# Choosing experts by top-eight and index instructions, and a new order for the last token tile of a router

## The reference

```
x = x + mix @ w_out
xn2 = rmsnorm(x, norm2_g)
lg = xn2 @ rg_w + rg_b                      # 8 groups
grp = top_k(lg, 1)
le = (xn2 @ re_w + re_b).reshape(t, 8, 8)   # 64 experts
top_v, top_i = top_k(le[grp], 2)
gate = softmax(lg)[grp] * softmax(top_v)
eidx = grp * 8 + top_i
x = x + sum over the two of gate * expert(eidx, xn2)
y = rmsnorm(x, final_norm_g)
```

## Time and profile before

| | us |
|---|---|
| median of three runs | 1886.19 (1886.02 to 1888.94) |
| span of the profiled execution | 1886.5 |
| PE busy in the span | 1759.1 (93%) |
| VectorE, ScalarE, GpSimd busy | 598.8, 444.0, 230.5 |
| moved by DMA | 406.33 MB, 215 GB/s over the span |

### The profile page before, as it was taken

One profiled execution on the slowest core, in us unless ns is written; L12 is line 12 of the kernel. 1 busy time (PEld: TensorE's weight loads), 2 busy tenths in 40 slices (PEclk: granted clock), 3 DMA queues, 4 the chain that ended last, 5 costly groups with the idle time before them and its releaser, 6 DMA issues.

```text
span 1886.5 us, 27617 instructions
## 1 busy us (share of the span) xinstructions
PE 1759.1 (93%) x11500; PEld 1479.2 (78%) x11500; DVE 598.8 (32%) x1074; ACT 444.0 (24%) x782; POOL 230.5 (12%) x293
## 2 busy tenths in 40 slices
PE   8999999999999999999999999997988888887884
PEld 8999999998888888999999998886545444454441
DVE  5000102433233333166134438566222211111116
ACT  6221225532222222221132115111111111111113
POOL 0003300000011001000000000001222222222220
PEclk9999999999999999999999999998999999999996
DMA  4222233244345445357535244125999999999987
GB/s 154 93 93 94 77 99 101 94 155 151 111 137 178 150 122 193 126 180 270 183 137 197 88 162 147 68 73 208 384 419 419 419 420 419 418 418 419 420 331 286
DMA packets 159478, 406.33 MB, mean 215 GB/s; under 512 B 20341, under 2 KB 102133, under 8 KB 134778
## 3 DMA queue, kind: packets, MB, share of 16 engines
q1 hardware_dynamic: 137402, 344.22, 49.3%
q0 software_dynamic: 21952, 60.34, 8.4%
HBM read 340.62 MB, written 79.60 MB: 223 GB/s over the span
## 4 chain that ended last, share of the span: by engine, by line
PE 89%; issue 4%; DMA 3%; DVE 3%; DVEq 1%; ACT 0%; SPq 0%; ACTq 0%; POOLq 0%
PE ps L1933 17%; PE ps L1935 16%; PE ps L1934 16%; PE ps L2235 12%; PE ps L2131 8%; PE ps L2257 6%; PE ps L2222 2%; PE ps L2236 2%; PE ps L2246 1%; PE ps L2022 1%; PE ps L2032 1%; PE ps L2033 1%; PE ps L1946 1%; DMA SG<-feat 1%; PE ps L2169 1%
## 5 line engine op out<-in xcount | busy, mean ns | idle before, releaser
L1933 PE MATMUL ps<-XH,WH 128*128 128x384 f32 (+1 forms) x1152 | 382.7, 332 | 0.0
L1935 PE MATMUL ps<-XH,WL 128*128 128x384 f32 (+1 forms) x1152 | 377.0, 327 | 0.0
L1934 PE MATMUL ps<-XL,WH 128*128 128x384 f32 (+1 forms) x1152 | 376.9, 327 | 0.0
L2235 PE MATMUL ps<-E,XT 128*64 128x256 f32 x1024 | 249.8, 400 | 74.7 <-issue 73.8
L2236 PE MATMUL ps<-E,XT 128*64 128x256 f32 x1024 | 251.2, 401 | 0.0
L2235 PEld LDWEIGHTS ps<-E,XT 128*64 128x64 f32 x1024 | 142.4, 144 | 132.9 <-issue 82.4
L1933 PEld LDWEIGHTS ps<-XH,WH 128*128 128x128 f32 x1152 | 216.1, 188 | 17.0 <-issue 15.1
L1934 PEld LDWEIGHTS ps<-XL,WH 128*128 128x128 f32 x1152 | 216.4, 188 | 0.0
L1935 PEld LDWEIGHTS ps<-XH,WL 128*128 128x128 f32 x1152 | 216.2, 188 | 0.0
L1933 PE MATMUL ps<-WH,XH 128*128 128x256 f32 (+2 forms) x648 | 184.7, 285 | 4.7 <-DVE XL L1381 4.7
L1387 DVE TENSOR_TENSOR WL<-RAW,WH 128x2048 fp32r<-128x2048 f32 (+1 forms) x34 | 78.1, 2297 | 348.1 <-ACT WH L1113 348.0
(11 more groups left out here) (331 smaller groups left out, 2360.1 us busy)
## 6 DMA issues: line engine op xcount, KB each, us to landing
E<-in_exp_w_dram SPq DMA_DIRECT2D x192, 1024.0 KB, 21.3
RAW<-in_w_in_dram SPq DMA_DIRECT2D x29, 1024.0 KB, 7.8
feat<-OF POOLq DMA_DIRECT2D x20, 1088.0 KB, 8.3
SG<-feat SPq DMA_DIRECT2D x24, 544.0 KB, 4.7
tokd<-OT POOLq DMA_DIRECT2D x10, 1024.0 KB, 7.3
cbuf<-feat SPq DMA_DIRECT2D x16, 544.0 KB, 6.1
X<-in_x_prompt_dram SPq DMA_DIRECT2D x16, 512.0 KB, 3.8
VR<-tokd SPq DMA_DIRECT2D x32, 256.0 KB, 3.0
```

Of the source, the lines that this page charges most:

```text
L1933: pe.matmul(out, hi, mhi, start=start, stop=False)
L1934: pe.matmul(out, hi, mlo, start=False, stop=False)
L1935: return pe.matmul(out, lo, mhi, start=False, stop=stop)
L2235: pe.matmul(ps[0:BR, 2 + b, 0:DE], XT[b][:, turned(k), :], E1[s][:, 1, k, :], start=(k == 0), stop=(k == KD - 1))
```

## The change

It has four parts.

1. `best_two` finds the best group by `max` (the eight largest values of a row) and `max_index` (their positions), a copy of the first position to float, and a comparison. The two experts come from one `max` and one `max_index` over the 64 masked logits, a copy of the first two positions, and one comparison for both one-hot rows. The maxima are kept in `gtop` and `etop`, which `gate_differences` reads. Indices are now counted from 1000 in `slf` rather than from -1000 in `iom`, so `look_up` adds without a constant. `look_up` handles both choices in one product and one reduction.
2. The norm of the last tile: ScalarE copies the transposes first, then does Square and Sqrt; VectorE does the reciprocal alone (`last_root`); ScalarE scales the rows by it into `sq4`, and GpSimd multiplies by the gain into N2 (`gain_last`) and stores them. Before, one VectorE instruction did both.
3. The logits of the last tile go to bank 4 (`logit_bank`), and do not wait for the ranks of tile 7 to be read (`r_rk`).
4. On TensorE `ranks(7)` now stands ahead of `router(8)`. Ten products of the identity stand before `ranks(8)` and eight between it and `slots(8)`, beside the 24 there were.

```
+        def logit_bank(n):
+            return 2 if n < NT - 1 else out_bank(NT - 2)
...
-            for n in range(NT):
+            for n in range(NT - 1):
                 store_n2(n)
+
+            def gain_last():
+                pool.wait_ge(x2_rms, NT + 1)
+                pool.wait_ge(n2_st[0], 16 * (NT // 2))
+                pool.tensor_tensor(N2[0][0:NDEC].rearrange("t (k p) -> t p k", k=KD), sq4[0:NDEC].rearrange("t (p k) -> t p k", k=KD),
+                                   g2b[0:NDEC].rearrange("t (p k) -> t p k", k=KD), ALU.mult)
+                pool.drain().then_inc(n2_ready, 1)
+            gain_last()
+            pool.wait_ge(n2_ready, NT + 1)
+            store_n2(NT - 1)
...
+            def norm2_last():
+                n = NT - 1
+                act.wait_ge(n2_tp, n + 1)
+                act.wait_ge(l_mm, n)
+                act.activation(NTt[:, :, 0:NDEC], ps[:, 0:2, :].rearrange("p b (k t) -> p (b k) t", k=4)[:, :, 0:NDEC], ACT.Copy).then_inc(n2_tc, 1)
+                act.activation(sq4[0:NDEC], X2[0:NDEC, n, :], ACT.Square, accum_out=ss4[0:NDEC])
+                act.drain()
+                act.activation(rt4[0:NDEC], ss4[0:NDEC], ACT.Sqrt, bias=epsc[0:NDEC], scale=1.0 / D).then_inc(x2_rms, 1)
+                act.wait_ge(n2_ready, NT)
+                act.activation(sq4[0:NDEC], X2[0:NDEC, n, :], ACT.Copy, scale=rs4[0:NDEC]).then_inc(x2_rms, 1)
...
             def best_two(n):
...
-                dve.tensor_reduce(gmx[:, n, :], lg, AX.X, ALU.max)
-                dve.drain()
-                first_best(gmn[:], lg, gmx[:, n, :], g8[:], GROUPS)
-                dve.tensor_scalar(g8[:], iom[:, 0:GROUPS], gmn[:], -1.0, ALU.is_equal, ALU.add)
-                dve.drain()
...
+                dve.max(out=gtop[:, n, :], in_=lg)
+                dve.drain()
+                dve.max_index(out=i8[:], in_max=gtop[:, n, :], in_values=lg)
+                dve.drain()
+                dve.tensor_copy(gmn[:], i8[:, 0:1])
+                dve.drain()
+                dve.tensor_scalar(g8[:], slf[:, 0, 0:GROUPS], gmn[:], -1.0, ALU.is_equal, ALU.add)
+                dve.drain()
...
-                for k in range(2):
-                    dve.tensor_reduce(v12[:, k, n:n + 1], le[:], AX.X, ALU.max)
-                    dve.drain()
-                    first_best(ek[:, k, n:n + 1], le[:], v12[:, k, n:n + 1], tm[:], NE)
-                    dve.tensor_scalar(oh[:, k, n, :], iom[:, 0:NE], ek[:, k, n:n + 1], None, ALU.is_equal)
-                    dve.drain()
-                    if k == 0:
-                        dve.scalar_tensor_tensor(out=le[:], in0=oh[:, 0, n, :], scalar=-2e30, in1=le[:], op0=ALU.mult, op1=ALU.add)
-                        dve.drain()
+                dve.max(out=etop[:, n, :], in_=le)
+                dve.drain()
+                dve.max_index(out=i8[:], in_max=etop[:, n, :], in_values=le)
+                dve.drain()
+                dve.tensor_copy(ek[:, :, n], i8[:, 0:2])
+                dve.drain()
+                dve.tensor_tensor(oh[:, :, n, :], slf[:, 0:1, 0:NE].to_broadcast([P, 2, NE]), ek[:, :, n:n + 1].to_broadcast([P, 2, NE]), ALU.is_equal)
+                dve.drain()
...
             def look_up(n):
                 dve.wait_ge(r_mm, n + 1)
-                for k in range(2):
-                    dve.tensor_tensor((tm, le)[k][:], oh[:, k, n, :], ps[:, 2, P:P + NE], ALU.mult)
-                dve.drain()
-                for k in range(2):
-                    last = dve.tensor_reduce(rk[:, k, n:n + 1], (tm, le)[k][:], AX.X, ALU.add)
-                last.then_inc(r_rk, 1)
+                dve.tensor_tensor(le2[:], oh[:, :, n, :], ps[:, 2:3, P:P + NE].to_broadcast([P, 2, NE]), ALU.mult)
+                dve.drain()
+                dve.tensor_reduce(rk[:, :, n], le2[:], AX.X, ALU.add).then_inc(r_rk, 1)
...
+            def last_root():
+                dve.wait_ge(x2_rms, NT)
+                dve.reciprocal(rs4[0:NDEC], rt4[0:NDEC])
+                dve.drain().then_inc(n2_ready, 1)
...
                 if n == NT - 1:
                     look_up(n - 1)
-                resid_norm(n)
+                    last_root()
+                else:
+                    resid_norm(n)
...
-                if n:
+                if 0 < n < NT - 1:
                     pe.wait_ge(r_rk, n)
                 for k in range(KD):
-                    last = pe.matmul(ps[0:rows, 2, 0:GROUPS + NE], NTt[:, k, 0:rows], wr[:, k, :], start=(k == 0), stop=(k == KD - 1))
+                    last = pe.matmul(ps[0:rows, logit_bank(n), 0:GROUPS + NE], NTt[:, k, 0:rows], wr[:, k, :], start=(k == 0), stop=(k == KD - 1))
...
+            def keep_clock(n):
+                for i in range(n):
+                    pe.matmul(ps[:, 6, 0:P], ident[:], ident[:], start=True, stop=True)
+            ranks(NT - 2)
             router(NT - 1)
-            ranks(NT - 2)
             logits(NT - 1)
             slots(NT - 3)
             slots(NT - 2)
+            keep_clock(10)
             ranks(NT - 1)
+            keep_clock(8)
             slots(NT - 1)
             pe.wait_ge(r_msk, NT + 1)
             pe.matmul(ps[:, 7, P:P + NE], onesm, cum[NT % 2][:], start=True, stop=True).then_inc(r_mm, 1)
-            for i in range(24):
-                pe.matmul(ps[:, 6, 0:P], ident[:], ident[:], start=True, stop=True)
+            keep_clock(24)
```

More of the change, by code:

```diff
@@ L7 @@
 I32 = mybir.dt.int32
+U32 = mybir.dt.uint32
 ALU = mybir.AluOpType
@@ L89, in trunk @@
         lgt = keep("lgt", [P, NT, GROUPS + NE])
+        gtop = keep("gtop", [P, NT, 8])
+        etop = keep("etop", [P, NT, 8])
         tidx = keep("tidx", [P, NBLK], I32)
@@ L244, in trunk @@
         cum = [sb(f"cum{i}", [P, NE]) for i in range(2)]
-        le = sb("le", [P, NE])
-        tm = sb("tm", [P, NE])
+        le2 = sb("le2", [P, 2, NE])
+        le = le2[:, 0, :]
         g8 = sb("g8", [P, GROUPS])
+        i8 = sb("i8", [P, 8], U32)
         iob = sb("iob", [P, NBLK], I32)
@@ L250, in trunk @@
         iop = sb("iop", [P, 1], I32)
-        gmx = sb("gmx", [P, NT, 1])
-        v12 = sb("v12", [P, 2, NT])
         ek = sb("ek", [P, 2, NT])
@@ L1319, in norm2 @@
                 act.activation(NTt[:, :, 0:rows], ps[:, 0:2, :].rearrange("p b (k t) -> p (b k) t", k=4)[:, :, 0:rows], ACT.Copy).then_inc(n2_tc, 1)
-            for n in range(NT):
+            def norm2_last():
[8 more added lines that the diff above has]
+                act.activation(sq4[0:NDEC], X2[0:NDEC, n, :], ACT.Copy, scale=rs4[0:NDEC]).then_inc(x2_rms, 1)
+            for n in range(NT - 1):
                 norm2(n)
+            norm2_last()
             def silu(st):
@@ L1654, in logit_bias @@
                 dve.wait_ge(l_mm, n + 1)
-                dve.scalar_tensor_tensor(out=lgt[0:rows, n, :], in0=ps[0:rows, 2, 0:GROUPS + NE], scalar=rs4[0:rows], in1=rb[0:rows], op0=ALU.mult, op1=ALU.add)
+                dve.scalar_tensor_tensor(out=lgt[0:rows, n, :], in0=ps[0:rows, logit_bank(n), 0:GROUPS + NE], scalar=rs4[0:rows], in1=rb[0:rows], op0=ALU.mult, op1=ALU.add)
                 dve.drain().then_inc(l_ready, 1)
-            def first_best(out, vals, best, scratch, n):
-                dve.scalar_tensor_tensor(out=scratch, in0=vals, scalar=best, in1=iom[:, 0:n], op0=ALU.is_equal, op1=ALU.mult)
-                dve.drain()
-                dve.tensor_reduce(out, scratch, AX.X, ALU.min)
-                dve.drain()
             def best_two(n):
@@ L1668, in best_two @@
                     dve.wait_ge(r_c, 1)
-                dve.tensor_reduce(gmx[:, n, :], lg, AX.X, ALU.max)
+                dve.max(out=gtop[:, n, :], in_=lg)
                 dve.drain()
-                first_best(gmn[:], lg, gmx[:, n, :], g8[:], GROUPS)
-                dve.tensor_scalar(g8[:], iom[:, 0:GROUPS], gmn[:], -1.0, ALU.is_equal, ALU.add)
+                dve.max_index(out=i8[:], in_max=gtop[:, n, :], in_values=lg)
                 dve.drain()
-                dve.scalar_tensor_tensor(out=le[:].rearrange("p (g e) -> p g e", g=GROUPS), in0=g8[:].rearrange("p (g a) -> p g a", a=1).to_broadcast([P, GROUPS, EPG]),
+                dve.tensor_copy(gmn[:], i8[:, 0:1])
+                dve.drain()
+                dve.tensor_scalar(g8[:], slf[:, 0, 0:GROUPS], gmn[:], -1.0, ALU.is_equal, ALU.add)
+                dve.drain()
+                dve.scalar_tensor_tensor(out=le.rearrange("p (g e) -> p g e", g=GROUPS), in0=g8[:].rearrange("p (g a) -> p g a", a=1).to_broadcast([P, GROUPS, EPG]),
                                          scalar=1e30, in1=lx.rearrange("p (g e) -> p g e", g=GROUPS), op0=ALU.mult, op1=ALU.add)
                 dve.drain()
-                for k in range(2):
-                    dve.tensor_reduce(v12[:, k, n:n + 1], le[:], AX.X, ALU.max)
-                    dve.drain()
-                    first_best(ek[:, k, n:n + 1], le[:], v12[:, k, n:n + 1], tm[:], NE)
-                    dve.tensor_scalar(oh[:, k, n, :], iom[:, 0:NE], ek[:, k, n:n + 1], None, ALU.is_equal)
-                    dve.drain()
```

(11 more changed lines are left out.)

## The result

The changed kernel takes 1880.7 us (median of 8 runs, 1880.13 to 1882.11) against 1886.43 us (median of 8, 1884.85 to 1889.17): 5.7 us less, ratio 0.9966 with a 95% interval of 0.9957 to 0.9975. The forecast was 1884.2 and its range ended at 1882.2. The direction was right; the size was wrong by almost three times, and, as the experiments show, nearly all of the gain is none of the things that were added up for it. The span of the profiled execution is 1878.9 us; that execution took 1880.67. In every run on record the span is 1.7 to 1.9 us shorter than the time, so the profiled execution of the kernel before, with its span of 1886.5, took some 1888.3 us: about 2 us above its median, and not 0.3. The two profiles differ by 1.9 us more than the medians do.

A forecast was written before the change was run, and what follows sets the result against it. The expert weight stream bounds the kernel from about 1302 us; x = 1.6 + 0.5 = 2.1 us closes 2.0 us of its 2.4 us hole, taking the span from 1886.5 to 1884.5 and the median to 1884.2 us, range 1882.2 to 1887.0.

The forecast's parts named there:

- The bound: TensorE sets the time before 1298 us, the expert weight stream from about 1302 us; the stream has a 2.4 us hole.
- This is the only idle time of the bound resource that an earlier first expert can remove.: Hole in the weight stream between 1330.5 and 1344 us: 2.4 us empty, 3.8 us as outer limit.
- The fourth rival: The change does not do what it says; time follows the weight stream's rate, 2.4 us either way; chance 0.07.
- Logits and bias, 2.0 us.: Last tile: the bias instruction starts at about 1303.1 instead of 1305.14, 2.0 us earlier, the largest single term.
- Choice of experts.: Last tile, bias to mask sum: 11 instructions for 15, 3.8 us instead of 4.80, 1.7 us saved with the old hold.
- The hold.: GpSimd's multiply holds VectorE's group-index copy 1.9 us; memsets hold the second copy 0.2; 2.1 of 3.7 us go back.
- Identity products, 0.5 us.: TensorE before the last ranks and slots: a higher clock could bring up to 1.1 us; 0.5 taken.
- The store.: Last tile's store leaves at about 1306.5, lands at 1312.9; the gather, at about 1315.5, is covered by 2 us.
- x: Time saved between 1298 and 1317 us, last residual sum to first gather: 1.6 + 0.5 = 2.1 us.
- the third rival: Slower: a long GpSimd multiply delays the mask and last store, which gates the gather; 1887.7 to 1888.7 us, chance 0.07.
- Expert 0 at 0 us.: Expert 0's first product after an idle TensorE: up to 1.7 us lost or won by the clock; 0 taken.
- Tiles 0 to 7 at 0.: Fewer VectorE instructions per tile, but TensorE is busy throughout the 14.50 us tile: worth 0.

The follow-up runs named there:

- experiment 8: The changed kernel, but GpSimd multiplies the last tile by the gain before the root is known and ScalarE scales N2 in place afterwards: 1878.5 us, ratio 0.9955.
- experiment 9: Experiment 8 with 37 instead of 24 identity products behind the last ranks: 1878.92 us, ratio 0.9959.
- experiment 14: Experiment 8 with the four gather buffers moved up by 192 bytes to start at a multiple of 256: 1878.24 us, ratio 0.9952.
- experiment 2: The kernel before with an unused tile of 576 bytes per partition in place of the two new tables, nothing else changed: 1880.84 us, ratio 0.9962.
- experiment 5: The kernel before with the ring of expert weights alone moved up by 64 bytes, to a multiple of 256: 1880.66 us, ratio 0.9969.
- experiment 10: The changed kernel without the ten and the eight new identity products: 1880.73 us, ratio 0.9964.
- experiment 1: The changed kernel with an unused tile of 448 bytes per partition, putting the weights' ring back at its old remainder modulo 512: 1887.28 us, ratio 0.9998.
- experiment 7: The changed kernel with the last tile's norm back on VectorE as one instruction, transposes still copied first on ScalarE: 1879.05 us, ratio 0.9962.

## Why the prediction was wrong

*The bound.* Right. The weight stream sets the time from 1302 us on, a hole of some 2.4 us follows the first reload, and an earlier first expert wins it (experiments 8, 9 and 14). That it can't win more is not shown. The size of 2.4 us was that of one profile: with the same instruction order the DMA share in the 10.7 us behind the reload was 0.69 in experiment 2 and 0.95 in experiment 5, by the clock of expert 0's first product.

*"This is the only idle time of the bound resource that an earlier first expert can remove."* It holds as far as the runs show, but the sum then took the rate of the stream as given, and that is the step that failed. The change adds two tables to the tiles that lie beneath everything, and moves the weights' destination by 576 bytes onto a multiple of 256. This term, worth 5.8 us (experiment 5) to 7.2 us (experiment 2), was not in the list of parts at all: it was put at nothing without a reason. What the runs showed is a stream whose 8 KB rows are 1.4% shorter. The fourth rival allowed for a changed rate with "0.5% of rate is 2.4 us either way" and a chance of 0.07, but took it for chance and named no cause; the rate differed by 1.25%. The added `keep` lines were in the diff.

*Logits and bias, 2.0 us.* 1.98 measured.

*Choice of experts.* The chain from bias to mask sum takes 5.07 us with a hold of 1.61 (1.84 less the 0.23 of its fellows), so 3.46 without; 3.5 to 4.1 was said and 3.8 taken. The count was uneven: the fifteen instructions of before leave out the clearing of the mask, the eleven of the new chain have it in; counted alike, ten at 0.32 give 3.2. max_index is two instructions, MATCH_VALUE_LOAD of 92 ns and FIND_INDEX8 of 160 to 219, which follow each other without a drain.

*The hold.* 1.9 us was said, 1.61 measured, but of another instruction. The copy of the index (one element from uint32) ran at its usual 0.15 us in the middle of GpSimd's multiply; the comparison behind it was held to within 0.03 us of the multiply's end. The multiply took 2.37 us, 2.5 was said. The second hold, 0.2 on the second copy, did not come: the copy ended at 1306.28, before the memsets.

*Identity products, 0.5 us.* 0.9 at the index by experiment 10, none of it at the gather.

*The store.* This is where x went. It left 1.0 us later than said and landed in 7.6 us, not 6.4, so it was down at 16.8, where 14.6 was said. Its cover was gone, as the index was there at 14.9: 3.4 us earlier than before, not 2.1. Without this wait the gather could have left at about 15.9; the wait took 2 us of the 3.4. The mechanism of the third rival, the last store gating the gather, was at work without making anything slower.

*Expert 0 at 0 us.* Against the one profile of before the low clock cost 0.7 us; against the mean of the seven kernels with that order (5.97 us) it cost 1.3 to 1.6. With all of it x was 0.5 between the two profiles and nothing between the groups, and the change's own work comes to 0.4 us with 1.7 either way (experiment 1). That is where the 2 us went: into the store's landing and a TensorE that ran longer at the low clock. They are to be had (experiments 7 and 8).

*Tiles 0 to 7 at 0.* Right; nothing but the common shift shows there.

## What to carry to other kernels

When a stage is bound by loads into SBUF, look at the address modulo 256 of the tiles that it writes, and try a pad in front of them; here it was worth as much as the whole change. And whenever a change adds or resizes a tile, compare it with the old kernel moved by the same number of bytes: a gain that an unused tile brings as well belongs to the address. Before a fraction of a microsecond is read from two profiles, see how far profiles of one instruction order lie apart (here 3 us at the first reload). Behind that, an instruction taken off the critical chain is not free where its result is stored: follow the store to whoever waits for its landing.

## What the runs showed of the hardware

Weight rows of 8 KB loaded into SBUF tiles at a multiple of 256 bytes took 309.6 to 310.0 ns on average while the experts ran, at four other places 313.1 to 315.0 (276.1 to 276.3 and 279.2 to 280.9 ns over all packets of the queue). In the first 27 us of the same stream most took 310 ns or less at either place.

GpSimd's multiply of two SBUF tensors also held a VectorE instruction with two SBUF inputs of two elements each. This is VectorE in experiment 8, where GpSimd multiplies from 1299.09 to 1301.46:

```profile
1299.45 0.29 DVE L1723 TENSOR_REDUCE rk<-le 128x2 f32<-128x128 f32 x1
1299.83 1.64 DVE L1727 TENSOR_TENSOR row<-ek,rk 128x2 f32<-128x2 f32 x1
```

It took 1.64 us instead of 0.16, while the reduction of one input beside the same multiply took its usual 0.29. This agrees with the second kind of the lock that the Trainium skill ("SBUF — State Buffer", "SBUF: two separate sides") names and that no row of before showed. The name of an instruction does not tell whether it is held: the cast of one element above was not, beside a multiply, while the cast of two elements (L1703) took 0.50 us beside a GpSimd memset in experiment 8 and 0.17 elsewhere.
